# A differential attention stage in which mixing runs one unit later, head outputs are evicted by ScalarE, and two weight splits and two output units are reordered

## What is computed

```python
def diff_attention(x, w_in, q_gain, k_gain, lq1, lk1, lq2, lk2, subln, w_out, lambda_init):
    q, k, v = jnp.split(x @ w_in, [2 * H * dh, 4 * H * dh], axis=-1)
    q = rmsnorm(q.reshape(B, T, H, 2, dh), q_gain) * (dh ** -0.5)
    k = rmsnorm(k.reshape(B, T, H, 2, dh), k_gain)
    v = v.reshape(B, T, H, 2 * dh)
    ...
    for s in range(0, T, QBLOCK):
        e = s + QBLOCK
        sc = jnp.einsum('bqhcd,bkhcd->bhcqk', q[:, s:e], k[:, :e]).astype(F32)
        sc = jnp.where(dist >= 0, sc - slopes[:, None, None, None] * dist, -jnp.inf)
        p = jax.nn.softmax(sc, axis=-1)
        pd = p[:, :, 0] - lam * p[:, :, 1]
        outs.append(jnp.einsum('bhqk,bkhe->bqhe', pd.astype(v.dtype), v[:, :e]))
    o = rmsnorm(jnp.concatenate(outs, axis=1), subln) * (1.0 - lambda_init)
    return o.reshape(B, T, H * 2 * dh) @ w_out
```

## Time and profile before

| | |
|---|---|
| median of 3 runs | 1671.21 µs |
| lowest and highest run | 1670.47 and 1676.15 µs |
| the profiled execution | 1677.7 µs |
| its span | 1675.9 µs |
| mean granted TensorE clock over the span | 0.962 of full speed |
| attention, first extreme to last weighing | 1165.78 to 1253.76 µs of the span |
| output units | 1270.08 to 1314 µs of the span |

### The profile page before, as it was taken

How to read it: one execution, slowest core, us unless ns; L and a number is a source line. 1 busy time by engine, 2 the same in 40 slices (tenths; PEclk the granted TensorE clock), 3 DMA queues, 4 the chain that set the end, 5 groups by cost and what they waited for, 6 DMA issues and landing times. The chain is left out here.

```text
span 1675.9 us, 18970 instructions
## 1 busy us (share of the span) xinstructions
PE 1546.4 (92%) x7317; PEld 1256.8 (75%) x7317; DVE 789.6 (47%) x932; ACT 672.3 (40%) x848; POOL 78.1 (5%) x60
## 2 busy tenths in 40 slices
PE   8999999998899989999999997998777849999996
PEld 7888888887675578888888886887456638888885
DVE  5433333223563325333332225343763359888884
ACT  4322222113433323322221124334652237787774
POOL 0000000000000000000000000000130011122111
PEclk9999999999999999999999998999888869999998
DMA  5222222221220031322223322321100389999993
GB/s 216 76 98 83 94 100 101 101 101 50 90 87 1 1 113 51 120 84 96 100 100 101 101 76 79 105 87 47 51 1 1 116 345 351 390 388 386 378 392 105
DMA packets 35729, 224.69 MB, mean 134 GB/s; under 512 B 5175, under 2 KB 5431, under 8 KB 11344
## 3 DMA queue, kind: packets, MB, share of 16 engines
q1 hardware_dynamic: 30912, 210.54, 33.4%
q0 software_dynamic: 4608, 13.22, 3.4%
q10 hardware_dynamic: 144, 0.03, 0.0%
HBM read 213.70 MB, written 13.63 MB: 136 GB/s over the span
## 5 line engine op out<-in xcount | busy, mean ns | idle before, releaser
L234 DVE TENSOR_TENSOR WL<-raw,WH 128x2048 fp32r<-128x2048 f32 x93 | 212.9, 2291 | 453.2 <-ACT WH L229 453.2
L239 PE MATMUL PS<-AH,WL 128*128 128x512 f32 (+2 forms) x776 | 289.7, 373 | 6.2 <-DVE AL L383 4.3
L240 PE MATMUL PS<-AL,WH 128*128 128x512 f32 (+2 forms) x776 | 289.0, 372 | 0.0
L241 PE MATMUL PS<-AH,WH 128*128 128x512 f32 (+2 forms) x776 | 289.0, 372 | 0.0
L229 ACT ACTIVATE WH<-raw 128x2048 fp32r<-128x2048 f32 x93 | 177.3, 1908 | 249.7 <-PE PS L241 247.2
L2201 DVE TENSOR_TENSOR WEL<-eraw,WEH 128x2048 fp32r<-128x2048 f32 x96 | 216.7, 2286 | 17.1 <-ACT WEH L2139 17.1
L2139 ACT ACTIVATE WEH<-eraw 128x2048 fp32r<-128x2048 f32 x96 | 181.6, 1912 | 19.8 <-PE PS L241 18.8
L239 PEld LDWEIGHTS PS<-AH,WL 128*128 128x128 f32 (+1 forms) x776 | 146.5, 189 | 32.9 <-DVE AL L383 4.5
L240 PEld LDWEIGHTS PS<-AL,WH 128*128 128x128 f32 (+1 forms) x776 | 146.6, 189 | 25.8
L241 PEld LDWEIGHTS PS<-AH,WH 128*128 128x128 f32 (+1 forms) x776 | 146.4, 189 | 25.4
L239 PE MATMUL PS<-WH,AL 128*128 128x512 f32 (+1 forms) x384 | 149.5, 389 | 12.5 <-DVE WL L234 8.8
(11 more groups left out here) (322 smaller groups left out, 2182.6 us busy)
## 6 DMA issues: line engine op xcount, KB each, us to landing
eraw<-experts SPq DMA_DIRECT2D x96, 1024.0 KB, 13.0
raw<-stream SPq DMA_DIRECT2D x94, 1024.0 KB, 4.8
moe_rows<-moe_rows_g SPq DMA_DIRECT2D x5, 512.0 KB, 14.2
X<-x SPq DMA_DIRECT2D x4, 512.0 KB, 6.4
out<-X SPq DMA_DIRECT2D x1, 2048.0 KB, 20.2
ffn_row<-rows SPq DMA_DIRECT2D x2, 512.0 KB, 9.5
final_row<-rows SPq DMA_DIRECT2D x2, 512.0 KB, 5.6
pool_bands<-band SPq DMA_DIRECT2D x1, 544.0 KB, 8.1
```

What stands on the lines that cost most here:

```text
L234: dve.tensor_tensor(WL[:, u % SLOTS, :], raw[:, u % SLOTS, :], WH[:, u % SLOTS, :].bitcast(F32), ALU.subtract).then_inc(unit_lo, 1)
L239: pe.matmul(acc, lhs_lo, rhs_hi, start=start, stop=False)
L240: pe.matmul(acc, lhs_hi, rhs_lo, start=False, stop=False)
L241: return pe.matmul(acc, lhs_hi, rhs_hi, start=False, stop=stop)
```

## The change

In `da_attend` the mix, the turn, the copy and the weighing of a unit each come one iteration later (i - 6 and i - 7 in place of i - 5 and i - 6), and the factors of a head in iteration 4(h + 1) + 2. The loops are one iteration longer.

`head_out` moves from DVE to ACT: in iteration i = 4h' + 3 ACT evicts head h' - 2. For the last head POOL and its halvings are left out; DVE takes four products with a sum (`tensor_tensor_reduce`, one per query tile, one operand from PSUM and one from `O`) after ACT's eviction.

The split of `U_DA_OUT` moves out of the attention loop into block b = 5 of `da_in`: on ACT behind the tile t = 0, on DVE behind transpose 11. The split of `U_DA_OUT + 1` moves from iteration 7 to iteration 9 on ACT and 13 on DVE. In `da_out` PE takes unit 2 for tiles 0 and 1 as soon as unit 2 is split, then waits for unit 3 and takes unit 3 for tiles 0 and 1, then tiles 2 and 3.

```diff
                         if b == 5:
                             qk_out(8 + 2 * t)
+                            if t == 0:
+                                split_hi(act, U_DA_OUT)
...
+                    if n == 11:
+                        split_lo(dve, U_DA_OUT)
...
-                for i in range(N + 6):
+                for i in range(N + 7):
                     if i + 1 < N:
                         scores(i + 1)
-                    if 0 <= i - 5 < N:
-                        turn(i - 5)
                     if 0 <= i - 6 < N:
-                        weigh(i - 6)
+                        turn(i - 6)
+                    if 0 <= i - 7 < N:
+                        weigh(i - 7)
...
             @block.scalar
             def _(act):
-                for i in range(N + 5):
+                def head_out(h):
+                    act.wait_ge(weighed, T * (h + 1))
+                    act.activation(head_cols(h), PS[:, 6 + h % 2, :].rearrange("p (q d) -> p q d", q=T), ACT.Copy
+                                   ).then_inc(heads_out, 1)
+
+                for i in range(N + 6):
...
-                    j = i - 5
+                    j = i - 6
...
-                    if i in (3, 7):
-                        split_hi(act, U_DA_OUT + i // 4)
+                    if i % T == 3 and i // T >= 2:
+                        head_out(i // T - 2)
+                    if i == 9:
+                        split_hi(act, U_DA_OUT + 1)
+                head_out(H - 1)
 
             @block.vector
...
-                for i in range(N + 5):
+                for i in range(N + 6):
...
-                    if q == 1 and 1 <= h <= H:
+                    if q == 2 and 1 <= h <= H:
...
-                    j = i - 5
+                    j = i - 6
...
-                    if i in (3, 7):
-                        split_lo(dve, U_DA_OUT + i // 4)
-                    if q == 2 and h >= 3:
+                    if i == 13:
+                        split_lo(dve, U_DA_OUT + 1)
+                    if q == 3 and h >= 3:
                         sum_squares(h - 3)
-                    if q == 2 and h >= 2:
-                        head_out(h - 2)
                 sum_squares(H - 2)
-                head_out(H - 1)
-                sum_squares(H - 1)
+                dve.wait_ge(heads_out, H)
+                dve.wait_ge(squared, H - 1)
+                last = PS[:, 6 + (H - 1) % 2, :].rearrange("p (q d) -> p q d", q=T)
+                for q in range(T):
+                    dve.tensor_tensor_reduce(head_junk[:, q, :], last[:, q, :], head_cols(H - 1)[:, q, :], 1.0, 0.0,
+                                             ALU.mult, ALU.add, stat[:, 0, q, H - 1:H]).then_inc(squared, 1)
 
             @block.gpsimd
             def _(pool):
-                for h in range(H):
+                for h in range(H - 1):
...
+                pe.wait_ge(unit_lo, u0 + 3)
+                unit_into(2, 0)
+                unit_into(2, 1)
                 pe.wait_ge(unit_lo, u0 + 4)
-                for t in range(T):
-                    mm = unit_into(2, t)
-                    if t == T - 1:
-                        mm.then_inc(unit_used, 1)
-                    mm = unit_into(3, t)
-                    mm.then_inc(made if t < T - 1 else unit_used, 1)
+                unit_into(3, 0).then_inc(made, 1)
+                unit_into(3, 1).then_inc(made, 1)
+                unit_into(2, 2)
+                unit_into(3, 2).then_inc(made, 1)
+                unit_into(2, 3).then_inc(unit_used, 1)
+                unit_into(3, 3).then_inc(unit_used, 1)
...
-                dve.wait_ge(squared, H)
+                dve.wait_ge(squared, H - 1 + T)
```

## The result

The changed kernel takes 1643.87 µs (median of 4 runs, 1641.63 to 1646.37) against 1671.57 (1670.47 to 1676.15): a ratio of 0.983 with a 95% interval of 0.9803 to 0.9856. Run again later it took 1647.60 (1641.52 to 1648.21) against 1671.78, ratio 0.9853 (0.9837 to 0.9869).

A forecast was written before the change was run, and what follows sets the result against it. PE, busy 92% of the span, was taken as the bound, so only its waits and lower clock counted. Terms -20.8, -1.1, -1.7 and -7.0 sum to -30.6 µs, from median 1671.21 to 1641; range 1633 to 1651.

The forecast's parts named there:

- The loop: Steady attention heads: 7.3 µs per head, from 8.50 at full clock and about 10.1 at the lower clock.
- The walk: Steady head: PE's next turn ready 1.85 µs after the scores, against 1.6 of PE work, leaving 0.25 bare.
- the drain: Iterations after the last extremes in attention: 9.0 µs instead of 10.11, a gain of 1.1.
- The split at iteration 13: Unit 1's low part on DVE, head 3: 2.2 µs more work, 0.8 hidden by slack, costing 1.4.
- Rival C: Attention loop: weight splits only move their stall; unit 1's costs 4.7 µs again instead of 2.0, total 1644; chance 0.05.
- The first split: Output unit 0's split, moved out of heads 0 and 1: idle ACT and DVE time takes it, cost 0.
- Last head: Between attention and norm, after the last weighing: 2.3 µs against 4.0, a gain of 1.7.
- Output units: Output stage: PE's 4.4 µs wait for unit 3 and the slow matmuls after it go, a gain of 7.0.
- Rival A: Heads 3 to 7: the lower clock stays, each losing 1.6 µs, 8 more, total 1649; chance 0.12.
- B: Attention loop: pitch stays near 8.5 µs through ACT or POOL contention, 7 more, total 1648; chance 0.08.
- D: Attention loop: waits have another cause than the lag, no loop gain, total 1662 or no change; chance 0.03.
- E: First score to end of first output unit: PE stays at 1.2 GHz, heads 11.3 µs, total 1679; chance 0.02.

The follow-up runs named there:

- the kernels without POOL: Kernel before, with later iterations only, and with head output on ACT only, each with POOL's operations cut to one column: 1664.99, 1661.37 and 1661.62 µs.
- run 10: Not a label: "this run" is the profiled run of the changed kernel, 1646.1 µs; 10 counts its slow products.
- the lag alone: Kernel before with only mix, turn, copy and weighing one iteration later, DVE keeping the head output copy: 1669.66 µs, ratio 0.9994.
- the eviction alone: Kernel before with only the head's output moved from DVE to ACT: 1680.12 µs, ratio 1.0058.

## Why the prediction was right, and where it was off

- **The loop.** Forecast 7.2 plus 0.1 for POOL; measured 7.36, with the bare wait at 0.33 for 0.25. The walk (the extremes of width 512 and the mix of 256 on DVE, against 1.6 of PE work) is confirmed by the wait's place, and its form for the kernels without POOL gave 7.97, 7.8 and 7.97 for 7.98, 7.81 and 7.98. What it didn't see is how much hangs on where POOL's squares fall: I priced that at 0.1 as if it were a small extra; it is 0.5 to 0.8 per head wherever it meets the mix that PE waits for, and in the changed kernel lag and eviction together move it away. The 0.1 wasn't worked out from where the squares would fall, so its fit is in part luck. The Trainium skill ("SBUF — State Buffer", section "SBUF: two separate sides") has a mix wait for the whole of a GpSimd operation that got the ports first. The trace agrees nearly: the mix of 0.61 that started with POOL's 1.04 took 1.44, 0.83 more.
- **Attention as a whole.** 88.0 to a forecast of 66.0; 66.1 measured. That they meet within 0.1 is luck: head 1 took 4.88 (6.0 forecast), head 2 8.80 (9.4) and the drain 8.33 (9.0), while head 3 took 9.61 (8.7) and head 4 8.74 (7.3), and the misses cancel. The split at iteration 13 was under-priced: PE waited 1.94, not 1.4, as the low part itself took 3.13 beside POOL, and the lower clock followed (in head 4 of this profile; in the second profile heads 3 and 4 took 10.83 and 7.50, the same sum). Rival C (4.7 again) is out. The first split found room, as forecast: attention starts at 1164.3 and 1163.1 in the two profiles, and between 1162.9 and 1166.2 in the profiles without the move.
- **Last head.** 6.75 to 4.86 between the last weighing and the first transposes, 1.9 for 1.7.
- **Output units.** The wait and the slow matmuls behind it are gone. From first product to last sum 52.77 became 47.11, 5.7 less and not 7.0: in this run 10 products at the head of the stage were slow, against 3 in the profile that I read and 9 in the second one of the kernel before. (The stage before ended at 1321.6, not at 1314 as the table ahead of the prediction has it.)
- **What was off** is the step from the profile to the median ("against the median of 1671.21 the same difference gives 1640.6"). The profiled run was one with three falls of the clock in the loop, 10.1 for 8.5, and a fourth in the drain, and the sum counted removing them as gain. In the kernel before run again the same stage takes 81.8; against 64.6 and 66.1 in the two profiles of the changed kernel that is 15.7 to 17.2, not 21.9. With 1.9, and 5.9 to 8.0 in the output units, the difference is 23.5 to 27.1. The medians show 24.2 and 27.7; that the first of these comparisons came within 2.9 of the forecast is helped by scatter of this size.
- **Rival A** holds in part: the lower clock is still there in heads 2 and 4 of one profile and in heads 3 and 4 of the other, but in neither in the steady heads. A swing such as the Trainium skill describes ("TensorE: Matmul & The Clock Gate", section "A second HAM failure mode: psum-queue depth-cycling") was seen in the kernel before in one profile of two, and in none of six steady heads of the changed kernel with waits of 0.33; that it has the cause named there is not shown. **B** was a real danger in another form: the lag alone (8.39) and the eviction alone (8.81 and more) both stay near B's 8.5. **D and E** are out.

## What to carry to other kernels

Before costing a stage, compare the profiled run's time with the median: where it is slower, find what it has more of, and don't count its removal as gain. Where GpSimd works beside VectorE operations with two SBUF operands, write down which of them it meets, and whether TensorE waits behind that one; moving an operation to an idle engine can move the meeting and lose time, as the eviction alone did (+9.5 µs, most of it at the lower clock behind a longer wait). Parts of a software pipeline can't be valued one at a time: here four parts came to 3.3 µs apart and 27.7 together.

## What was not expected

The block works both ways: a POOL operation of 0.73 took 2.65 µs beside a low part on DVE, which itself took 3.13 for 2.29. And the clock differs between executions of one program. In one profile of the changed kernel 10 products behind the norm were slow, and in the other none, after the same 4.9 µs of idle PE. There the clock fell too, but once, and the lower stretch lay over the transposes and ended before the first product; these are the transposes of that profile:

```profile
1232.52:1241.79 9.27, 6.96 (x32) 6.17 (x33) 6.31 (x6) 3.34 (x3) 0.00 (x0) 0.52 0.01 2
```

What decides where the lower stretch lies stays open.
